# Last norm of a two-block transformer kernel: two of its eight output tiles through GpSimd and ScalarE, from a second spread of the factor

## The reference

```python
def rmsnorm_2(x, g):
    x32 = x.astype(jnp.float32)
    inv = lax.rsqrt(jnp.mean(x32 * x32, axis=-1, keepdims=True) + EPS)
    return (x32 * inv).astype(x.dtype) * g
...
        x = x + jnp.einsum("bsd,de->bse", merged, w_out[l])

    return rmsnorm_2(x, norm_f_g)
```

## Time and profile before

| what | value |
|---|---|
| median of 3 runs | 1749.23 us |
| lowest, highest run | 1746.66, 1750.09 us |
| the profiled execution's own time | 1748.27 us |
| its span, first to last instruction | 1746.6 us |
| mean granted TensorE clock, share of full speed | 0.981 |
| busy: TensorE, VectorE, ScalarE, GpSimd | 95%, 62%, 41%, 5% |

### The profile page before, as it was taken

How to read it: one execution, slowest core, us unless ns; L and a number is a source line. 1 busy time by engine, 2 the same in 40 slices (tenths; PEclk the granted TensorE clock), 3 DMA queues, 4 the chain that set the end, 5 groups by cost and what they waited for, 6 DMA issues and landing times.

```text
span 1746.6 us, 25469 instructions
## 1 busy us (share of the span) xinstructions
PE 1657.2 (95%) x9800; PEld 1327.6 (76%) x9800; DVE 1080.0 (62%) x1682; ACT 718.5 (41%) x1084; POOL 90.9 (5%) x130
## 2 busy tenths in 40 slices
PE   5979999999999999999989999999999999998997
PEld 2768777888888868777668888888886778765786
DVE  8799877665566765665655554455775564746444
ACT  4433434332333344444443332333546674644331
POOL 0063210000000000000000000000000000000000
PEclk9989999999999999999989999999999999999998
DMA  8342662334443535342222222322321221211231
GB/s 351 98 113 75 229 217 97 144 132 158 167 144 126 164 132 182 109 145 85 70 79 96 96 78 90 120 96 69 102 98 69 73 73 52 84 59 48 65 116 48
DMA packets 48821, 198.79 MB, mean 114 GB/s; under 512 B 8112, under 2 KB 13072, under 8 KB 35424
## 3 DMA queue, kind: packets, MB, share of 16 engines
q1 hardware_dynamic: 36064, 154.52, 25.5%
q0 software_dynamic: 12672, 43.10, 7.2%
HBM read 192.71 MB, written 4.23 MB: 113 GB/s over the span
## 4 chain that ended last, share of the span: by engine, by line
PE 81%; DVE 6%; ACT 5%; issue 5%; DMA 2%; POOL 1%; SPq 1%; DVEq 0%; ACTq 0%; POOLq 0%
PE ps L523 24%; PE ps L524 24%; PE ps L525 24%; ACT w_hi L981 2%; PE ps L628 2%; PE ps L641 2%; PE ps L653 2%; DMA ada<-in_ada_k 1%; PE ps L796 1%; DVE w_lo L1451 1%; ACT pw L1090 1%; POOL Mtz L340 1%; PE ps L772 0%; PE ps L712 0%; ACT sq L1081 0%
## 5 line engine op out<-in xcount | busy, mean ns | idle before, releaser
L523 PE MATMUL ps<-xn_hi,w_lo 128*128 128x512 f32 x1248 | 500.5, 401 | 13.7 <-DVE xn_lo L1594 9.6
L525 PE MATMUL ps<-xn_hi,w_hi 128*128 128x512 f32 x1248 | 489.8, 392 | 0.0
L524 PE MATMUL ps<-xn_lo,w_hi 128*128 128x512 f32 x1248 | 489.6, 392 | 0.0
L1451 DVE TENSOR_TENSOR w_lo<-raw,w_hi 128x2048 fp32r<-128x2048 f32 (+4 forms) x147 | 311.8, 2123 | 199.1 <-ACT w_hi L981 198.9
L981 ACT ACTIVATE w_hi<-raw 128x2048 fp32r<-128x2048 f32 (+4 forms) x147 | 260.9, 1775 | 177.9 <-PE ps L525 165.6
L523 PEld LDWEIGHTS ps<-xn_hi,w_lo 128*128 128x128 f32 x1248 | 236.6, 190 | 70.9 <-issue 18.9
L525 PEld LDWEIGHTS ps<-xn_hi,w_hi 128*128 128x128 f32 x1248 | 236.3, 189 | 50.7
L524 PEld LDWEIGHTS ps<-xn_lo,w_hi 128*128 128x128 f32 x1248 | 236.7, 190 | 45.4
L525 PE MATMUL ps<-act_hi,w_hi 128*128 128x512 f32 x352 | 136.9, 389 | 0.0
L523 PE MATMUL ps<-act_hi,w_lo 128*128 128x512 f32 x352 | 136.9, 389 | 0.0
L524 PE MATMUL ps<-act_lo,w_hi 128*128 128x512 f32 x352 | 136.9, 389 | 0.0
(11 more groups left out here) (395 smaller groups left out, 2428.6 us busy)
## 6 DMA issues: line engine op xcount, KB each, us to landing
raw<-in_weights SPq DMA_DIRECT2D x95, 1024.0 KB, 4.9
adaw<-in_ada_w POOLq DMA_DIRECT2D x64, 512.0 KB, 4.7
raw<-in_weights SPq DMA_DIRECT2D x18, 768.0 KB, 4.2
raw<-in_weights SPq DMA_DIRECT2D x16, 640.0 KB, 3.9
ada<-in_ada_k SPq DMA_DIRECT2D x8, 1024.0 KB, 17.8
rot<-in_ada_w POOLq DMA_DIRECT2D x16, 512.0 KB, 5.0
fbias<-f_dram SPq DMA_DIRECT2D x16, 256.0 KB, 4.1
raw<-in_weights SPq DMA_DIRECT2D x8, 512.0 KB, 3.5
```

What stands on the lines that cost most here:

```text
L523: pe.matmul(bank, lo_w, hi_x, start=start, stop=False)
L524: pe.matmul(bank, hi_w, lo_x, start=False, stop=False)
L525: return pe.matmul(bank, hi_w, hi_x, start=False, stop=stop)
L1451: V.tensor_tensor(w_lo[:, slot, w], raw[:, slot, w], f32(w_hi[:, slot, w]), ALU.subtract).then_inc(split_lo, 1)
```

## The change

`norm_spread` makes, for the norm `out` alone, four more transposes of the same factors into bank 6, before the one semaphore that VectorE waits for. VectorE writes six tiles and not eight. ScalarE copies bank 6 to `sq[:, 0]`; GpSimd multiplies `h[:, 6]` and `h[:, 7]` by it into `fin`; ScalarE multiplies each of these by the gain, in place. SyncE's store of the fourth pair waits for that instead of for VectorE.

```diff
     rope_t, kr_ready, mq_side, mk_rope = sem("rope_t"), sem("kr_ready"), sem("mq_side"), sem("mk_rope")
+    rs_side, fin_prod, fin_side = sem("rs_side"), sem("fin_prod"), sem("fin_side")
...
         for m in range(0, DT, 2):
-            sp.wait_ge(norm_t, NTILE["out"] + m + 2)
+            if m < 6:
+                sp.wait_ge(norm_t, NTILE["out"] + m + 2)
+            else:
+                sp.wait_ge(fin_side, 2)
             sp.dma_start(out[m * P:(m + 2) * P].rearrange("(m p) t -> p m t", p=P), fin[:, m:m + 2]).then_inc(out_saved, 16)
...
         pool.dma_start(ropt[64:P, :], rope).then_inc(in_rope, 16)
+        pool.wait_ge(rs_side, 1)
+        for m in (6, 7):
+            nc.gpsimd.tensor_tensor(fin[:, m], h[:, m], sq[:, 0], ALU.mult).then_inc(fin_prod, 1)
...
                 mm = pe.transpose(ps[:, 7, t * P:(t + 1) * P], rcol[:, t:t + 1].to_broadcast([P, P]), ident[:])
+            if name == "out":
+                for t in range(QBLK):
+                    mm = pe.transpose(ps[:, 6, t * P:(t + 1) * P], rcol[:, t:t + 1].to_broadcast([P, P]), ident[:])
...
         norm("out")
+        act.wait_ge(rstd_out, NIDX["out"] + 1)
+        A(sq[:, 0], ps[:, 6], ACT.Copy).then_inc(rs_side, 1)
+        for m in (6, 7):
+            act.wait_ge(fin_prod, m - 5)
+            A(fin[:, m], fin[:, m], ACT.Copy, scale=pcol("norm_f_g", m)).then_inc(fin_side, 1)
...
-            for m in range(n):
+            for m in range(6 if name == "out" else n):
                 to = norm_buf(m) if hi is not None else dst(m)
                 V.scalar_tensor_tensor(to, src(m), scale(m), ps[:, bank], ALU.mult, ALU.mult).then_inc(norm_t, 1)
```

## The result

The changed kernel takes 1751.85 us (median of 12 runs, 1748.28 to 1756.42), the kernel before 1747.9 in the 12 runs now compared (1745.0 to 1750.23). The ratio is 1.0019, with a 95% interval of 1.0010 to 1.0028: 3.3 us slower, 1.7 to 4.9 (the two medians are 3.95 apart). The ratio is just inside the 0.2% up to which the prediction speaks of no change, though its interval leaves out 1. The time lies inside the forecast's range and the sign is the forecast's, but 0.94 us of cost was expected and 3.3 were measured. The rest of this text is about the 2 us between.

What follows compares the result with a forecast made beforehand. The prediction took the never-pausing stream of final stores as the bound; four extra transposes start it 0.94 us later, all else adds nothing: 1749.23 + 0.94 = 1750.2 us, range 1747.6 to 1752.3.

Steps and rivals of the forecast that it cites:

- The stream of stores: At the kernel's end, output stores run unpaused for 5.50 us at 381 GB/s; their start sets the end; chance 0.80.
- the pace of 436 GB/s: Skill's rate for the final stores: stream 4.8 us, change costing some 0.2 us instead of 0.9; not adopted.
- the rival that followed the last pair: At the end, the fourth store's issue sets the end: no change, 1749.2, or 1748.7 with short transposes; chance 0.10.
- The transposes: In the last norm's spread, four more at the low clock delay VectorE's first tile and the stores by 0.94 us.
- The lower bound of 0.43: Least cost in us of the four extra transposes, from a second spread at 2.4 GHz starting 0.43 after the first.
- The side way: Tiles 6 and 7 through ScalarE and GpSimd, done at 1742.6; fourth store still issued near 1743.2, no cost.
- The lock between VectorE and GpSimd: In the last norm, the two engines shut each other out; fourth store 2.8 us later, 1752.0; chance 0.05.
- A late first product on GpSimd: GpSimd, idle since 832, starts tile 6 late: 0.10 to 11.44 us, at most 1759.9, 1754.5 by the skill; chance 0.05.
- The step that failed: After the fourth store, only SyncE's wait for all four stores was taken to be queued; no further cost.
- The slower rival: GpSimd's late start on its first product, slower by over 0.2% from 4.3 us on; chance 0.05, 0.04 of it slower.
- the slack of the stores: At the fourth store, tiles 6 and 7 may be late by 1.1 us, or 1.7 from their own end, without cost.

Runs made afterwards that it cites:

- all-mended kernel: Changed kernel plus a GpSimd drain at 832 us, VectorE's semaphore raised by the first four transposes: 10.14 us from reciprocal to end, ratio to before 0.9991.
- one tile: Changed kernel with only tile 7 made by GpSimd and ScalarE, VectorE writing seven: 12.01 us from reciprocal to end, ratio to before 1.0005.
- changed, drained early: Changed kernel with a drain of GpSimd's own added at 832 us, where it is idle: 11.06 us from reciprocal to end, ratio to before 1.0009.
- late wait: Kernel before, with one GpSimd wait for VectorE's eighth output tile and nothing behind it: 14.77 us from reciprocal to end, ratio to before 1.0029.
- late clearing, drained early: Kernel before, GpSimd draining at about 832 us, then clearing one column after VectorE's eighth tile: 10.18 us from reciprocal to end, ratio 0.9997.

## Why the prediction was right, and where it fell short

- *What bounds the end of the kernel before: right.* The stream of stores, not VectorE's tiles, was named as the limit. The changed kernel's stream ran 5.52 us where 5.50 were expected, full throughout; the pace of 436 GB/s, by which the prediction had 4.8 us, did not come (the section of the Trainium skill that it cites for it, DMA: Bandwidth & Descriptors, "Anatomy of one DMA", is on transfers that GpSimd issues, and these stores are SyncE's). The all-mended kernel is the direct proof, and the rival that followed the last pair loses: it would have had the end 0.6 us sooner there, or the landing unmoved in the changed kernel, where it moved from 9.8 to 10.6 with the fourth issue no later. The end of the changed kernel itself, though, was set by neither (below).
- *The transposes: right in mechanism, 0.94 expected, 0.76 measured.* The first of the eight caught part of the time at the high clock, which is 0.09 of it; the rest is the pace, for with all eight at 1.2 GHz the four more cost 0.85 (one tile; changed, drained early), 0.21 each and not 0.235. The lower bound of 0.43 was wrongly built. At 2.4 GHz the second spread did add 0.43, but there the first takes 0.65 and not 1.12, so against the kernel before the cost was -0.03. What was not seen is that the clock of the spread changes between executions, though TensorE's program is the same.
- *The side way: right.* ScalarE's copy 0.60 (0.59 expected), the products 1.26 each (1.2), the multiplies 0.72 (0.71), done 3.9 us after VectorE's first tile began (3.8), and the fourth store went out 6.6 us after the reciprocal (6.8). No table load showed.
- *The lock between VectorE and GpSimd: rightly held small.* VectorE's six tiles took 4.04 us beside GpSimd's products (4.05 expected without a lock).
- *A late first product on GpSimd: it did not come.* After 909 us of idleness the first product began 0.08 us after ScalarE's copy. The Trainium skill, GPSIMD Engine Reference, "Instruction dispatch", has a first call of a freshly loaded routine at about 6 us; no such load shows in any run here.
- *The step that failed* is the path to the end of the program. The prediction followed it through SyncE's queue alone: "Even without any stream limit, then, the last pair gains nothing. Behind it only the wait for all four stores is queued." What stands behind the new work on GpSimd it did not ask, and the words on the kernel before have nothing queued there. But behind GpSimd's products stood its closing drain, 7.64 us beyond them, and the whole program waits for it. The sum put that term at nothing without a reason. With it taken out by the early drain the stretch is 11.06: so 13.11 - 11.06 = 2.05 us are the drain's, what the stores' end does not cover of its 7.64, and 11.06 - 10.16 = 0.90 the transposes' (the changed kernel's own first tile came 0.09 sooner than in that run, which shifts as much from one to the other). The sum that was needed, 2.95, lies within the interval of the runs, 1.7 to 4.9. That the range held the time is luck. Its upper end, 1752.3, comes from the lock, which did not happen; and the sum was laid on 1749.23, the median of three runs, where twelve have 1747.9. On the base that the forecast used, 3.3 us would have given 1752.5.
- *The slower rival* put a price on the right engine and the right cover, GpSimd late and the slack of the stores, but at its start instead of at its end.

## What to carry to other kernels

An engine that has long finished is not free at the end of a program: ask what its closing instructions cost, and read them in the trace of before, where they lie hidden; a drain of its own, put where the engine is idle, may pay the price ahead of time. When the output is stored while it is being made, compare the time of the stores' stream with the time of the work: once they are nearly equal, relief of the work is worth nothing, and only an earlier or smaller first store moves the end. A chain of waits that ends in a compute engine, with microseconds of span behind it, has not shown the limit. And a term read at one clock holds for that clock only: here the price of four transposes went from nothing to 0.85 us with the moment at which the clock fell.

## What the runs showed of the hardware that was not expected

- GpSimd's first drain lasts 7.58 us when nothing is left to execute (late wait), 7.7 with a clearing of 0.10 us in front, and 10.14 with 2.49 us of products; right behind its last DMA issue (0.55 us) it lasts 9.75 (before) or 10.0 (late clearing, drained early). The second drain of the same program lasts 0.17 (2.60 with the 2.49 us of products). The closing drains of the other engines last hardly longer than the work in front of them: ScalarE 0.75 for an instruction of 0.72, VectorE 4.07 for 4.04.
- TensorE's granted clock falls from 2.4 to 1.2 GHz near the end of the kernel in every execution profiled here, but in the sums in some, and between root and spread, within the spread or behind it in others; eight matmuls put into the idle time did not keep it up (0.95 of full speed in the window from 1735.5, 0.50 from 1736.0).
- Stores of 256 KB run at the same 380 GB/s or so as stores of 512 KB, and one lands 2.1 us after its issue instead of 2.9 to 3.0.
